# Four short stages before an expert layer: 3 banks for the gate logits, keys taken ahead of the mask, head 0 turned and lambda made one stage earlier, norm sums and the first expert weights made in the output product

## What is computed

```python
xn   = rmsnorm(concat([meta, x]), ln1_w)
dq, dk, dv, gq, gk, gv, gr, zf, zb = split(xn @ w_in)
lam  = exp(sum(q1 * k1)) - exp(sum(q2 * k2)) + lam_init
# differential attention: 4 heads, each with two query/key halves of 64
s    = einsum('bqhcd,bkhcd->bhcqk', rope(dq) * 64 ** -0.5, rope(dk))
p    = softmax(s)
da   = rmsnorm((p[:, :, 0] - lam * p[:, :, 1]) @ dv, da_subln_w) * (1 - lam_init)
# gated linear attention in chunks of 64, forwards and backwards
g_f, g_b = log_sigmoid(zf @ w2_f + b_f) / 16, log_sigmoid(zb @ w2_b + b_b) / 16
go   = rmsnorm(gla(gq, gk, gv, g_f) + gla_reversed(gq, gk, gv, g_b), gla_norm_w) * silu(gr)
h    = (h + concat([da, go]) @ w_out)[16:]
# experts: 8 heads pick 16 of 16384 experts for each token
hn   = rmsnorm(h, ln2_w)
q    = hn @ w_q
h    = h + sum_k gate_k * gelu(hn . u[idx_k]) * v[idx_k]
```

## Time and profile before

| what | us |
|---|---|
| time before, median of 3 runs | 2654.69 (2650.17 to 2654.87) |
| the profiled execution: its time | 2648.79 |
| the profiled execution: span from first to last instruction | 2647.0 |
| PE busy | 2582.6 (98% of the span) |
| DVE busy | 1530.2 (58%) |
| POOL busy | 1026.9 (39%) |
| ACT busy | 925.0 (35%) |
| mean granted clock of PE | 0.989 |

### The profile page before, as it was taken

One profiled execution on the slowest core, in us unless ns is written; L12 is line 12 of the kernel. 1 busy time (PEld: TensorE's weight loads), 2 busy tenths in 40 slices (PEclk: granted clock), 3 DMA queues, 4 the chain that ended last, 5 costly groups with the idle time before them and its releaser, 6 DMA issues.

```text
span 2647.0 us, 33693 instructions
## 1 busy us (share of the span) xinstructions
PE 2582.6 (98%) x12573; PEld 2118.5 (80%) x12573; DVE 1530.2 (58%) x3293; ACT 925.0 (35%) x1472; POOL 1026.9 (39%) x683
## 2 busy tenths in 40 slices
PE   8999889999999999999999999999999999999998
PEld 7776678888888888888888888877977788788886
DVE  3234736999688522225888888843974445433322
ACT  4223533333344322223333333453334442422222
POOL 4320110389888888604777777210350000000000
PEclk9998999999999999999999999999999999999999
DMA  4210046755657766658999999832332123333321
GB/s 155 72 32 33 33 126 211 241 127 137 148 124 195 195 144 145 147 164 288 376 370 366 373 370 370 308 105 80 86 90 56 41 83 132 87 97 96 96 96 72
DMA packets 330946, 427.87 MB, mean 162 GB/s; under 512 B 58720, under 2 KB 246912, under 8 KB 330272
## 3 DMA queue, kind: packets, MB, share of 16 engines
q1 hardware_dynamic: 271392, 358.39, 41.9%
q0 software_dynamic: 59392, 67.34, 10.4%
HBM read 362.59 MB, written 63.05 MB: 161 GB/s over the span
## 4 chain that ended last, share of the span: by engine, by line
PE 82%; ACT 1%; DVE 1%; issue 1%; DMA 0%; SPq 0%; DVEq 0%; ACTq 0%
PE bank L209 26%; PE bank L213 26%; PE bank L212 26%; PE bank L2500 1%; PE bank L1688 1%; PE bank L2475 1%; PE bank L1671 1%; PE bank L2458 0%; PE bank L2498 0%; ACT s_wh L2219 0%; ACT s_junk L375 0%; PE bank L2488 0%; PE bank L475 0%; PE bank L2510 0%; DVE s_h L2814 0%
## 5 line engine op out<-in xcount | busy, mean ns | idle before, releaser
L1727 DVE TENSOR_TENSOR pe_wl<-pe_raw,pe_wh 128x1024 fp32r<-128x1024 f32 x272 | 354.5, 1305 | 367.1 <-ACT pe_wh L1587 350.6
L1517 POOL DMA_INDIRECT scratch_sums<-pe_pick,pe_cell_u x256 | 430.0, 1680 | 78.0 <-issue 77.5
L209 PE MATMUL bank<-pe_xh,pe_wh 128*128 128x512 f32 x1152 | 453.2, 393 | 1.3 <-DVE pe_xl L452 1.3
L213 PE MATMUL bank<-pe_xh,pe_wl 128*128 128x512 f32 x1152 | 448.6, 389 | 0.0
L212 PE MATMUL bank<-pe_xl,pe_wh 128*128 128x512 f32 x1152 | 448.5, 389 | 0.0
L1587 ACT ACTIVATE pe_wh<-pe_raw 128x1024 fp32r<-128x1024 f32 x272 | 288.0, 1059 | 304.2 <-PE bank L213 272.9
L2562 DVE TENSOR_TENSOR s_wl<-s_raw,s_wh 128x1024 fp32r<-128x1024 f32 x143 | 179.4, 1256 | 273.6 <-ACT s_wh L2219 272.3
L209 PE MATMUL bank<-pe_wh,pe_hh 128*128 128x512 f32 x768 | 298.8, 389 | 0.0
L212 PE MATMUL bank<-pe_wl,pe_hh 128*128 128x512 f32 x768 | 298.8, 389 | 0.0
L213 PE MATMUL bank<-pe_wh,pe_hl 128*128 128x512 f32 x768 | 298.8, 389 | 0.0
L209 PEld LDWEIGHTS bank<-pe_xh,pe_wh 128*128 128x128 f32 x1152 | 216.4, 188 | 46.4 <-issue 1.2
(11 more groups left out here) (452 smaller groups left out, 4652.6 us busy)
## 6 DMA issues: line engine op xcount, KB each, us to landing
pe_raw<-in_peer_u SPq DMA_DIRECT2D x128, 512.0 KB
pe_raw<-in_peer_v SPq DMA_DIRECT2D x128, 512.0 KB
scratch_hidden<-pe_a_out SPq DMA_DIRECT2D x128, 256.0 KB
pe_a_in<-scratch_hidden SPq DMA_DIRECT2D x128, 192.0 KB
s_raw<-in_w_in SPq DMA_DIRECT2D x48, 512.0 KB, 3.8
...
```

The costliest lines, as they stand in the source:

```text
L209: first = pe.matmul(out, lhs[0], rhs[0], start=start, stop=False, skip_group_check=skip)
L213: return pe.matmul(out, lhs[1], rhs[0], start=False, stop=stop, skip_group_check=skip)
L1517: pool.indirect_dma_start(cells, bass.IndirectOffsetOnAxis(ap=cell_u[:, t, at:at + 1], axis=0), pick[:, t, 2, at:at + 1], None, compute_op ...
L1727: dve.tensor_tensor(wl[:, i % RING, :], raw[:, i % RAW, :], wh[:, i % RING, :].bitcast(F32), ALU.subtract).then_inc(S["w_lo"], 1)
```

## The change

- Stage 1: the gate logits use three banks instead of two. Three are made before block gk, the other two after the first and the second slab of it.
- Stage 1: DVE takes block k out of its banks before it masks the last token tile, not after.
- Stage 1: lambda's products and its Exp are made after the decay's Exp, its end after the rotation of the keys.
- Stage 1: ACT squares the first three of `mix_g`'s four token tiles with row sums, one head at a time, two tiles ahead of the SiLU and one behind it. At the stage's end PE turns head 0's queries and keys into banks 0 and 4.
- Stage 2: only the last tile of `mix_g` is squared here. The meta keys and head 1 are turned first, heads 2 and 3 behind the scores of turns 0 and 1; the sum of squares and its root come before the turns. Banks are dealt out anew.
- Stage 3: PE waits for each of k-tiles 4 to 7 by itself. SP loads the first four slabs of expert query weights; ACT squares each half of `h` with row sums, and ACT and DVE split two of the slabs between the halves.
- Stage 4: the two sums are added, one root and one reciprocal serve all token tiles (`SummedStats`), and the loads and splits that stage 3 has made are gone.

The diff, without the allocation of buffers and semaphores, the bank in DVE's bias addition and the second half of the move of lambda (its old place):

```diff
--- before.py
+++ after.py
...
                 use(t)
+class SummedStats(RowStats):
+    def __init__(self, s, rows, halves):
+        self.rows, self.meta, self.width, self.halves = rows, None, rows.shape[2], halves
+        self.tiles, self.order = NT, list(range(NT))
+        self.ss, self.root, self.rstd = s.sb("n_ss", [P, NT]), s.sb("n_root", [P, NT]), s.sb("n_rstd", [P, NT])
+        self.meaned, self.rooted = s.sem("n_mean"), s.sem("n_root")
+    def on_scalar(self, act, ready):
+        act.wait_ge(self.meaned, 1)
+        act.activation(self.root[:, :], self.ss[:, :], ACT.Sqrt).then_inc(self.rooted, 1)
+    def on_vector(self, dve, chain, use, front=None):
+        chain(dve.tensor_tensor(self.ss[:, :], self.halves[:, 0, :], self.halves[:, 1, :], ALU.add))
+        dve.tensor_scalar(self.ss[:, :], self.ss[:, :], 1.0 / self.width, EPS, ALU.mult, ALU.add)\
+            .then_inc(self.meaned, 1)
+        dve.wait_ge(self.rooted, 1)
+        chain(dve.reciprocal(self.rstd[:, :], self.root[:, :]))
+        for t in range(NT):
+            use(t)
 class NormColumns:
...
-        self.stats = RowStats(s, rows, meta, junk=junk)
+        self.stats = RowStats(s, rows, meta, junk=junk) if halves is None else SummedStats(s, rows, halves)
...
             act.activation(decay_m[:, :], decay_m[:, :], ACT.Exp).then_inc(S["decayed"], 1)
+            act.wait_ge(S["lam_done"], 1)
+            act.activation(lam[:, :], lam_sum[:, :], ACT.Exp).then_inc(S["lam_exp"], 1)
...
+
+            def square_output(t):
+                act.wait_ge(S["o_taken"], 2 * t + 2)
+                for hd in range(GLA_HEADS):
+                    n = t * GLA_HEADS + hd
+                    act.activation(square[:, :], L["mix_g"][:, t, hd * GLA_DV:(hd + 1) * GLA_DV], ACT.Square,
+                                   accum_out=L["linear_ss"][:, n:n + 1]).then_inc(S["squared"], 1)
+                    act.wait_ge(S["squared"], n + 1)
             round_to(gr_b["slab0"] + SLOTS - 1)
+            for t in range(2):
+                square_output(t)
             act.wait_ge(gemm.bank_free, gemm.freed(gr_b))
             act.activation(L["gr"][:, :, :], L["gr"][:, :, :], ACT.Silu)
-            act.wait_ge(S["lam_done"], 1)
-            act.activation(lam[:, :], lam_sum[:, :], ACT.Exp).then_inc(S["lam_exp"], 1)
+            square_output(2)
...
             pe.wait_ge(gemm.bank_free, gemm.freed(zT_b))
-            for t, n in tiles:
-                if t >= 2:
-                    pe.wait_ge(S["y_taken"], t - 1)
+            def gate_logits(t):
+                n = tiles[t][1]
+                if t >= 3:
+                    pe.wait_ge(S["y_taken"], t - 2)
                 cols = slice(META + t * P, META + (t + 1) * P) if t < NT else slice(0, META)
-                pe.matmul(bank[0:n, SIDE + 1 + t % 2, :], L["zT"][rows96, 0, cols], w2[rows96, :], start=True, stop=True)\
+                pe.matmul(bank[0:n, SIDE + t % 3, :], L["zT"][rows96, 0, cols], w2[rows96, :], start=True, stop=True)\
                     .then_inc(S["z_done"], 1)
-            gemm.on_tensor(pe, gk_b)
+            for t in range(3):
+                gate_logits(t)
+            def logits_after(i):
+                if i < 2:
+                    gate_logits(3 + i)
+            gemm.on_tensor(pe, gk_b, between=logits_after)
...
             gemm.on_tensor(pe, gr_b, between=outputs_after)
+            pe.wait_ge(S["rotated"], 2)
+            pe.wait_ge(gemm.bank_free, gemm.freed(gr_b))
+            for b, src in ((0, L["q"]), (4, L["k"])):
+                for t in range(NT):
+                    pe.transpose(bank[:, b, t * P:(t + 1) * P], src[:, t, 0:P], ident)
...
             dve.tensor_tensor(km[:, :, :], km[:, :, :], L["gqk"][:, 2:4, 0:META], ALU.mult).then_inc(S["km_done"], 1)
+            dve.wait_ge(S["lam_landed"], 16 * 4)
+            dve.wait_ge(S["norm_w_landed"], 16)
+            for n in range(2):
+                chain(dve.tensor_tensor(lam_prod[:, n, :], lam_in[:, 2 * n, :], lam_in[:, 2 * n + 1, :], ALU.mult))
+            dve.tensor_reduce(lam_sum[:, :], lam_prod[:, :, :], AX.X, ALU.add).then_inc(S["lam_done"], 1)
...
-            for t in range(NT):
+            dve.sem_inc(S["rotated"], 1)
+            def mask_chunk(t):
...
                 dve.wait_ge(S["a_taken"], t + 1)
-                last = dve.tensor_tensor(fw, fw, bw, ALU.add)
-            chain(last)
+                return dve.tensor_tensor(fw, fw, bw, ALU.add)
+            for t in range(NT - 1):
+                mask_chunk(t)
             take(k_b)
+            chain(mask_chunk(NT - 1))
             dve.wait_ge(gemm.bank_free, gemm.freed(k_b))
             rotate(split(L["k"][:, :, :]), 0, NT, P)
+            dve.sem_inc(S["rotated"], 1)
             rotate(L["k_m"][:, :].rearrange("p (t h c) -> p t h c", t=1, h=8), NT, NT + 1, META)
+            dve.wait_ge(S["lam_exp"], 1)
+            chain(dve.tensor_tensor(lam[:, 0:1], lam[:, 1:2], lam[:, 0:1], ALU.subtract))
+            chain(dve.tensor_scalar(lam[:, 0:1], lam[:, 0:1], -LAM_INIT, None, ALU.add))
...
         LINEAR_FROM = 4
+        Q_BANK, K_BANK, KM_BANK = (0, 1, 7, 5), (4, 6, 4, 6), 5
...
         def _(act):
-            for hd in range(DA_HEADS):
-                act.wait_ge(q_turned, hd + 1)
-                act.activation(qT[:, hd, :], bank[:, hd, :], ACT.Copy, scale=DA_DIM ** -0.5).then_inc(q_ready, 1)
-            act.activation(sq[:, :, :].rearrange("p (t h) v -> p t h v", t=NT),
-                           mix_g[:, :, :].rearrange("p t (h v) -> p t h v", h=GLA_HEADS), ACT.Square)\
+            def take_query(hd):
+                act.wait_ge(q_turned, hd)
+                act.activation(qT[:, hd, :], bank[:, Q_BANK[hd], :], ACT.Copy, scale=DA_DIM ** -0.5).then_inc(q_ready, 1)
+            act.activation(qT[:, 0, :], bank[:, Q_BANK[0], :], ACT.Copy, scale=DA_DIM ** -0.5).then_inc(q_ready, 1)
+            act.activation(sq[:, :, :], mix_g[:, NT - 1, :].rearrange("p (h v) -> p h v", h=GLA_HEADS), ACT.Square)\
                 .then_inc(squared, 1)
+            take_query(1)
+            act.wait_ge(mean, 1)
+            act.activation(root[:, :], ss[:, :], ACT.Sqrt).then_inc(rooted, 1)
...
                     act.activation(aT[:, e % 2, :], bank[:, W_BANK + e % 2, :], ACT.Copy).then_inc(aT_ready, 1)
-                if r == 1:
-                    act.wait_ge(mean, 1)
-                    act.activation(root[:, :], ss[:, :], ACT.Sqrt).then_inc(rooted, 1)
...
                             .then_inc(exped, 1)
+                if r + 2 < DA_HEADS:
+                    take_query(r + 2)
...
                 last.then_inc(turned, 1)
+            def head_columns(hd):
+                columns(Q_BANK[hd], hd, q, q_turned)
+                columns(K_BANK[hd], hd, k, k_turned)
             ring.open_slots(pe)
             for hd in range(DA_HEADS):
-                columns(hd, hd, q, q_turned)
-                columns(DA_HEADS + hd, hd, k, k_turned)
-            pe.wait_ge(q_ready, 1)
-            for hd in range(DA_HEADS):
-                last = pe.transpose(bank[:, 0, hd * META:(hd + 1) * META], km[:, hd * P:(hd + 1) * P],
+                last = pe.transpose(bank[:, KM_BANK, hd * META:(hd + 1) * META], km[:, hd * P:(hd + 1) * P],
                                     ident[0:META, 0:META])
             last.then_inc(k_turned, 1)
-            pe.wait_ge(q_ready, DA_HEADS)
-            pe.wait_ge(k_ready, DA_HEADS + 1)
+            head_columns(1)
+            pe.wait_ge(q_ready, 2)
+            pe.wait_ge(k_ready, 2)
...
                                   kT[cc, hd, BANK:TM], start=True, stop=True).then_inc(scored, 1)
+                if r + 2 < DA_HEADS:
+                    pe.wait_ge(k_ready, 2 + r)
+                    head_columns(r + 2)
+                if r == 2:
+                    pe.wait_ge(q_ready, DA_HEADS)
+                    pe.wait_ge(k_ready, DA_HEADS + 1)
...
             chain = Chain(dve, vec)
-            for hd in range(DA_HEADS):
-                dve.wait_ge(k_turned, hd + 1)
...
+            def take_key(hd):
+                if hd:
+                    dve.wait_ge(k_turned, hd + 1)
+                dve.tensor_copy(kT[:, hd, META:TM], bank[:, K_BANK[hd], :]).then_inc(k_ready, 1)
             def norm_sums():
                 dve.wait_ge(squared, 1)
-                chain(dve.tensor_reduce(ss[:, :], sq[:, :, :], AX.X, ALU.add))
+                chain(dve.tensor_reduce(ss[:, (NT - 1) * GLA_HEADS:NT * GLA_HEADS], sq[:, :, :], AX.X, ALU.add))
...
                     .then_inc(maxed, 1)
+            take_key(0)
+            dve.wait_ge(k_turned, 1)
+            dve.tensor_copy(kT[:, :, 0:META],
+                            bank[:, KM_BANK, 0:DA_HEADS * META].rearrange("p (h m) -> p h m", m=META))\
+                .then_inc(k_ready, 1)
+            norm_sums()
+            take_key(1)
...
                     maximum(r, 1)
-                if r == 0:
-                    norm_sums()
+                if r + 2 < DA_HEADS:
```

(44 more changed lines are left out.)

50 lines of the change are left out of this document (25 added, 25 removed).

## The result

On the chip of the first comparison the changed kernel takes 2635.56 us (median of 4 runs, 2634.26 to 2638.76), the kernel before 2652.88 (4 runs, 2650.17 to 2654.87): a ratio of 0.9937, 95% interval 0.992 to 0.9954. On a second chip it was 2638.77 against 2649.62 (4 and 23 runs), a ratio of 0.996 (0.9945 to 0.9974), 10.9 us instead of 17.3. So there are two profiles of each kernel: "first" is the pair of the first comparison, "again" the pair of the second chip. The first profile of the kernel before is of an execution of 2648.79 us, none of the four. Spans: 2647.0 and 2634.3 first, 2647.2 and 2636.9 again.

A forecast was written before the change was run, and what follows sets the result against it. PE was taken to bound the kernel, so an earlier first expert product should reach the end. Six terms summed to 11.5 us (bounds 6.4 and 16.0); from the median 2654.7 the forecast was 2643, range 2633 to 2652.

The forecast's parts named there:

- logits, 3 banks: Stage 1: gate logits in three banks let block gk, then gv, start earlier; 2.7 us kept after a slab wait.
- keys ahead of the mask: Stage 1: DVE copies block k's tiles before the last mask, removing PE's wait for its banks; 2.9 us.
- opening: Start of the attention: fewer turns and passes before the first scores, root before the turns; turn 2 starts 2.3 us earlier.
- stage 3, wait: Stage 3: PE awaits only the first of four late columns, starting at 337.9 instead of 339.75; 1.8 us.
- stage 3, clock: Stage 3, behind PE's shortened wait: part of the loss at granted clock 0.50 disappears; 0.8 us, bounds 0 and 1.7.
- stage 4: Stage 4's opening: after the last sum, a shorter path brings the first turn from 378.82 to 377.8; 1.0 us.
- the first rival: Attention: PE, busier in the opening, keeps a better clock, gaining 7 us more, for 2636; chance 0.15.
- three to four turns: Attention: number of turns said to run at low clock before the change, 6.1 us each against 4.15 at 2.4 GHz.
- The passes wait for the fifth logit: Stage 1: ACT's Exp and Ln passes, ahead of rounding gv's second slab, await a logit no earlier than before; slab ready at 58.1.
- I take that loss as gone: Stage 1, start of block gk: the 1.4 us lost by running 2.8 us at 1.2 GHz would disappear.
- the two cases I had weighed: Attention's turn 2: 3.3 us earlier at full clock, or only 0.6 if the clock is already low from turn 1.
- Not reaching the end: Expert stage: DVE, nearly as full as PE, makes an item late and the gain is lost; 2654, chance 0.05.

## Why the prediction was right

| term | predicted (bounds) | measured |
|---|---|---|
| logits, 3 banks | 2.7 (1.2 to 3.8) | 0.0 |
| keys ahead of the mask | 2.9 | 2.9, and 1.4 to 2.8 of clock behind it in three profiles of four |
| opening | 2.3 (0.6 to 3.3) | 2.4 and 2.9 at the first scores; 2.0 and 3.7 by time |
| stage 3, wait | 1.8 | 1.7 |
| stage 3, clock | 0.8 (0 to 1.7) | at most 0.6, see below |
| stage 4 | 1.0 (-0.1 to 2.5) | 0.55 + 0.30 |

The waits at block k and in stage 3 came out as their rows said, and the sum without the clock, 0 + 2.9 + 2.9 + 1.7 + 0.85 = 8.4, stands under the forecast 11.5. The second pair's spans differ by 10.3, of which the clock behind the keys' wait is 2.8, the clock in stage 4's turns 1.0, and the attention's clock takes some back; the first pair's by 12.7, where the attention's clock gives most of the rest. The first pair's medians differ by 17.3 because the kernel before had its highest median there: 2652.88, against 2649.3 to 2650.5 in the four series of the experiments, and 2648.79 in its profiled execution. That the second chip's 10.9 comes so near to the 11.5 of the sum is luck: a term of 2.7 gave nothing, and a clock behind the keys' wait that no term held gave as much. The forecast was 2643 with a range from 2633 to 2652; 2635.56 lies in it, 7 below the forecast and close to the first rival's 2636. The better clock of that rival was there in the first pair (0.91 against 0.81), but that the opening keeps it up isn't shown: the same kernel gave 0.91 and 0.86. Its price also rested on "three to four turns" at the low clock; by the mean of 0.81 it was some 33 us, more than five turns.

Of the signs, these held: no wait for block k, one short wait in stage 3 (0.19), the first Exp 2.8 behind the first score, and less than 2 at gv's second slab. These didn't: gk started at 37.5, but its window had 0.79 and not 1.00; the first scores came 5.3 and 9.1 us earlier, not 8; the first expert product 13.8 and 10.8, not 11 to 12.

**The step that failed is the logits.** The prediction says "The passes wait for the fifth logit, which is no earlier than before", and then costs the slab as if it were no later either. It is done 6.4 later (47.3 against 41.0), since gk's second slab now stands ahead of it; Exp, which had not waited for it before, starts 2.5 later, and everything in ScalarE's queue behind Exp goes with it: the slab is ready at 61.2, not at 58.1. The second half was "I take that loss as gone" of the clock in gk: it was gone in four of nine profiles. And the two logits inside gk cost about 2.5, not 1.8 (an estimate: from gk to gv 14.15 at full clock, against 12.99 less 1.4 in the kernel before). So gv started 1.3 earlier behind the first logit, not 3.8. That PE's wait at the second slab, 1.08, is the 1.1 forecast is luck: the slab was wanted and was ready some 3 us later than predicted. Where the slab is rounded first and the clock holds, this part of stage 1 gives 2.9, about the 2.7 that was predicted.

**Opening.** First scores 2.9 earlier than by the old opening where 2.6 was forecast, turn 2 3.8 earlier where 2.3 was: the clock, full up to 239 us, was the better of the two cases I had weighed. What I missed is that 16 turns moved behind the first scores take part of it back. On the price of a table load the rows decide: a load of 1.28 us at 229.65, the root at 230.94, the next load at 231.17 and the Exp at 232.47, so two loads and the root cost 2.8, as forecast (232.4 + 2.8). The Trainium skill, ScalarE: Activation LUTs, What ACT_TABLE_LOAD costs, would add a drain of 1.38 us to each; this trace disagrees with it.

**Stage 3's clock.** Once the waits were gone the low stretch fell on the opening turns instead (312 to 315 us at 0.58): from the first turn to the first product 3.1 us, where the first profile of before had 2.1 and its second 3.1. Against the first of before the clock gave 0.6, against the second nothing.

**Stage 4.** The working adds up to 377.6, a gain of 1.2; it says 377.8 and 1.0. The edit gave 0.55 in front of the first product: in the changed kernel the last square ended 1.2 us behind the last sum (363.83 to 364.99, second profile), not 0.7. From the first turn to the first expert product it took 6.0 and 7.4 us before, 6.4 both times after; that is the clock again.

**Not reaching the end** is refuted: behind the first expert product the distance to the end changed by -1.1 and -0.5, and both profiles of the changed kernel have a low clock in 2256 to 2262 us (0.72 and 0.76) where both of the kernel before have 1.00.
